# Hybrid attention layer, gates stage: the score matmuls of the next head stand behind the value matmuls of a head

## What is computed

```python
h = rms_norm(x, attn_norm_g)
proj = h @ w_in      # q, k, v of 8 stick-breaking heads and of 8 sparse heads, index heads, gates
o_sb = stick_breaking_attention(q_sb, k_sb, v_sb)
o_ds = indexed_sparse_attention(rope(norm(q_ds)), rope(norm(k_ds)), v_ds, iq, ik, w_ix, topk=64)
merged = sigmoid(g_sb) * (o_sb @ w_branch[:SB_W]) + sigmoid(g_ds) * (o_ds @ w_branch[SB_W:])
x = x + merged @ w_out
u = causal_depthwise_conv(rms_norm(x, ffn_norm_g) @ w_up, conv_w, conv_b)
gate, val = split(u)
return x + (silu(gate) * val) @ w_down
```

## Time and profile before

| | us |
|---|---|
| median of 3 runs | 1438.19 (1438.11 to 1438.35) |
| the profiled execution's time | 1438.27 |
| its span in the trace | 1436.3 |
| PE busy | 1429.9 (100%) |
| DVE busy | 1140.8 (79%) |
| ACT busy | 841.9 (59%) |
| POOL busy | 448.6 (31%) |
| gates stage | 332.7 to some 537 |

### The profile page before, as it was taken

One profiled execution on the slowest core, in us unless ns is written; L12 is line 12 of the kernel. 1 busy time (PEld: TensorE's weight loads), 2 busy tenths in 40 slices (PEclk: granted clock), 3 DMA queues, 4 the chain that ended last, 5 costly groups with the idle time before them and its releaser, 6 DMA issues.

```text
span 1436.3 us, 23630 instructions
## 1 busy us (share of the span) xinstructions
PE 1429.9 (100%) x7570; PEld 1225.7 (85%) x7570; DVE 1140.8 (79%) x1533; ACT 841.9 (59%) x1181; POOL 448.6 (31%) x495
## 2 busy tenths in 40 slices
PE   9999999999999999999999999999999999999999
PEld 7888888888888888888888888888888888888887
DVE  6778998886656656889967777778778778999998
ACT  6645677566767766666665455454554545465553
POOL 2310000423232213650015455655556555200000
PEclk9999999999999999999999999999999999999999
DMA  8665665665554555567666666666666665576664
GB/s 250 188 191 169 204 201 179 201 182 173 158 174 146 173 164 183 183 222 236 187 183 183 190 192 188 178 191 190 199 185 182 188 192 189 193 232 206 201 208 147
DMA packets 121063, 272.24 MB, mean 190 GB/s; under 512 B 10688, under 2 KB 10976, under 8 KB 121008
## 3 DMA queue, kind: packets, MB, share of 16 engines
q1 hardware_dynamic: 119936, 268.99, 61.1%
q0 software_dynamic: 896, 2.42, 0.7%
q10 hardware_dynamic: 176, 0.14, 0.0%
HBM read 269.42 MB, written 2.10 MB: 189 GB/s over the span
## 4 chain that ended last, share of the span: by engine, by line
PE 98%; DVE 1%; DMA 0%; ACT 0%; issue 0%; SPq 0%; DVEq 0%; ACTq 0%
PE bank L2084 97%; DMA y<-in_x 0%; PE bank L2133 0%; DVE lo L1208 0%; PE bank L2345 0%; PE bank L2386 0%; ACT hT L652 0%; DVE y L1754 0%; PE bank L2213 0%; ACT hi L635 0%; DVE lo L1099 0%; DVE msum L1225 0%; DVE msum L1226 0%; ACT hi L713 0%; DVE msum L1235 0%
## 5 line engine op out<-in xcount | busy, mean ns | idle before, releaser
L1099 DVE TENSOR_TENSOR lo<-raw,hi 128x1024 fp32r<-128x1024 f32 (+1 forms) x343 | 446.1, 1306 | 167.3 <-ACT hi L635 166.7
L635 ACT ACTIVATE hi<-raw 128x1024 fp32r<-128x1024 f32 (+1 forms) x343 | 360.2, 1053 | 272.8 <-PE bank L2084 267.7
L2084 PE MATMUL bank<-h2T,hi 128*128 128x512 f32 x1408 | 483.3, 394 | 0.0
L2084 PE MATMUL bank<-h2T,lo 128*128 128x256 f32 x1408 | 376.8, 278 | 0.0
L2084 PEld LDWEIGHTS bank<-h2T,hi 128*128 128x128 f32 x1408 | 257.9, 188 | 53.5
L2084 PE MATMUL bank<-hT,hi 128*128 128x512 f32 (+1 forms) x784 | 273.7, 395 | 0.0
L2084 PEld LDWEIGHTS bank<-h2T,lo 128*128 128x128 f32 x1408 | 264.5, 188 | 7.8
L2084 PE MATMUL bank<-hT,lo 128*128 128x256 f32 (+1 forms) x784 | 213.0, 282 | 0.0
L2048 POOL TENSOR_TENSOR u<-u,rms_row 128x256 f32<-128x256 f32 x88 | 120.8, 1373 | 184.8 <-DVE u L1606 165.8
L2084 PE MATMUL bank<-hi,ffT 128*128 128x512 f32 x576 | 177.4, 389 | 0.0
L2084 PEld LDWEIGHTS bank<-hT,hi 128*128 128x128 f32 (+1 forms) x784 | 144.2, 187 | 29.7 <-DVE hT L1124 0.3
(11 more groups left out here) (299 smaller groups left out, 2025.3 us busy)
## 6 DMA issues: line engine op xcount, KB each, us to landing
raw<-in_w_up SPq DMA_DIRECT2D x176, 512.0 KB, 3.8
raw<-in_w_in SPq DMA_DIRECT2D x160, 512.0 KB, 3.6
raw<-in_w_down SPq DMA_DIRECT2D x88, 512.0 KB, 4.4
raw<-in_w_branch SPq DMA_DIRECT2D x32, 512.0 KB, 3.7
raw<-in_w_out SPq DMA_DIRECT2D x24, 512.0 KB, 5.2
raw4h<-in_w_in SPq DMA_DIRECT2D x8, 512.0 KB, 3.8
raw5h<-in_w_in SPq DMA_DIRECT2D x8, 512.0 KB, 4.1
y<-in_x SPq DMA_DIRECT2D x4, 512.0 KB, 6.6
```

The source lines that it names most:

```text
L635: act.activation(hi[s][:, 0:width], raw[s][:, 0:width], ACT.Copy)\
L1099: dve.tensor_tensor(lo[s][:, 0:width], raw[s][:, 0:width], hi[s][:, 0:width].bitcast(f32), ALU.subtract)\
L2084: return pe.matmul(o, l, r, start=start, stop=stop, skip_group_check=True)
```

## The change

The four score matmuls with their waits become a function, `head_logits`. Only head 0 still runs it behind its chunk 0. At the end of head h, behind the value matmuls, PE runs the scores of head h+1, for h = 0 to 6. The loop over heads is written as head 0, a loop over heads 1 to 6, and head 7. Nothing changes in the code of ACT, DVE, POOL and SP.

```diff
-            with pe.Fori(0, NH) as h:
+            def head_logits(h):
+                pe.wait_ge(staged_qk, 3 * h + 3)
+                pe.wait_ge(qkT_done, 8)
+                mm(B[0][:, 0:S], sb_k[:, 0:P], sb_q[:, :], True, True)
+                mm(B[0][:, S:KEYS], sb_k[:, P:S], sb_q[:, P:S], False, True)\
+                    .then_inc(z_full, 1)
+                mm(B[1][:, 0:P], ds_qk[:, 0:P], ds_qk[:, S:S + P], True, True)
+                mm(B[1][:, P:KEYS], ds_qk[:, P:S], ds_qk[:, S:2 * S], True, True)\
+                    .then_inc(logit_full, 1)
+
+            def gates_body(h, before, more):
...
-                    if j == 0:
-                        pe.wait_ge(staged_qk, 3 * h + 3)
...
+                    if j == 0 and not before:
+                        head_logits(h)
...
+                if more:
+                    head_logits(h + 1)
+
+            gates_body(0, False, True)
+            with pe.Fori(1, NH - 1) as h:
+                gates_body(h, True, True)
+            gates_body(NH - 1, True, False)
```

## The result

| | us |
|---|---|
| changed kernel, median of 6 runs | 1445.54 (1445.35 to 1446.39) |
| kernel before, median of 6 runs | 1438.14 (1437.38 to 1438.35) |
| ratio, 95% interval | 1.0054 (1.0044 to 1.0064) |
| span of the profiled execution, after and before | 1443.7 and 1436.3 |

A forecast was written before the change was run, and what follows sets the result against it. PE was taken as the bound, with 98% of the chain. Seven heads times 0.64 us of stall, 4.5 us, on the profiled 1438.27 gave 1442.8, less 0.08 for the median: 1442.7 us, range 1439.4 to 1445.4.

The forecast's parts named there:

- Slower, the likeliest outcome: Whole kernel: a time slower than 1441.1 us counts as slower; chance 0.74.
- Nothing saved by two stretches: PE, heads 1 to 7: seven fewer switches between kinds of matmul save 0 to 0.35 us in all; taken as 0.
- The shift: ACT after chunk 0: split of j=1 starts 1.31 us later; 0.95 us stay from the split of j=2 to `prob`.
- The margin of 0.14 us: PE's transposes: of 1.09 us between the second `prob` and the first weight load, the 0.95 us shift leaves 0.14.
- DVE ahead of POOL: Heads 1 to 7: DVE's split of j=4 follows `stay_lo` at once, 0.54 us ahead of POOL's second `prob`.
- can hold it up: DVE's split of j=4: the first `prob`, served after `stay_lo`, lengthens it by 0.23 us, bounds 0 and 0.53.
- the rival with both `prob` instructions behind the split: Transposes: DVE goes from `stay_lo` into the split without letting POOL in; 1.01 us a head, 1445.3 us; chance 0.06.
- The earlier trace: Rows used as price: a POOL instruction served between two back-to-back DVE splits; the second took 1.75 us, 0.53 more.
- Chunk 1 and all behind it keep their times: PE, heads 1 to 7: moving the scores ahead makes only chunk 0 end later, by 1.31 us.
- by the rule to the letter: Shared SBUF port: first `prob` holds the split until 398.71, stalling about 0.9 us a head, 6.2 us in all.
- the forecast's 0.64 us a head: Transposes, heads 1 to 7: PE's weight load starts at 400.44 instead of 399.80; bounds 0.41 and 0.94 us.

The follow-up runs named there:

- the waiting split: Changed kernel with one wait more on DVE: its split of j=4 waits until the first of POOL's two `prob` instructions is done; 1440.25 us.
- the last one: Changed kernel with DVE's j=4 split waiting for the first `prob`, plus an extra transpose in heads 0 to 6 and ahead of the branch stage; 1438.98 us.
- The late ACT: Kernel before, PE's order untouched, with four extra `abs` instructions on ACT ahead of `soft` in all 8 heads, results not used; 1446.10 us.
- The run with the gap: Changed kernel with four two-column reciprocals on DVE between `stay_lo` and the split of j=4, results not used; 1443.97 us.
- the run with `prob` on VectorE: Changed kernel with the scaling of `prob` moved from POOL to DVE, behind `stay_lo`; 1440.29 us.
- the remedies: Changed kernel with the waiting split, 1440.25 us; with a transpose ahead of the branch stage, 1444.69; in the heads, 1446.43; combined, 1439.20 and 1438.98.

## Why the prediction was wrong

The time, 1445.54 us, lies 0.14 us above the range of 1439.4 to 1445.4, less than the runs differ among themselves (one of the six, 1445.35, is inside); the forecast itself was 1442.7, 2.8 us lower. Slower, the likeliest outcome, came. By its steps:

- **Nothing saved by two stretches.** Right to 0.02 us a head: the best heads with the new order take 25.71 us against 25.73.
- **The shift.** 1.31 us at the split of j=1, 0.95 at that of j=2: right, and 0.93 at `prob`.
- **The margin of 0.14 us.** Right, measured in head 1 of the run with the waiting split, and again (0.14) in heads 2 to 7 of the last one.
- **DVE ahead of POOL.** Right: its split starts 15.35 us behind the values, forecast 15.36. The late ACT with the scores in their old place and the waiting split with the scores in the new one show that lateness and this order, not the place of the scores as such, make the wait.
- **The step that failed: that the first `prob` "can hold it up" and is served between `stay_lo` and the split.** The split was not held at all, and the first `prob` was: the rival with both `prob` instructions behind the split, to which I gave 0.06 and 1445.3 us. The earlier trace rows was the wrong row to lean on. There the POOL instruction, another operation, had been waiting 1.1 us; here it starts 0.17 us ahead of the split. The first `prob` takes 0.39 us from the split's end (398.66 + 1.22 to 398.49 + 1.77), and 0.72 alone. So by my estimate some 0.33 us pass from its start until it needs the port, by which time the split has it. The run with the gap fits: with the split 0.42 us behind its start, `prob` goes through. This is argued from lengths and not shown, and it holds for the first `prob`, which starts from idle. The second follows it without a pause, and the same working gives 0.13 us (0.92 alone, 0.79 from the split's end in head 0): it went through with only 0.09 us (before) and 0.14 us (waiting split) ahead of the split. A head lost 0.89 us by this, not 0.64: 7 x 0.89 = 6.2 of the 7.4 us.
- **"Chunk 1 and all behind it keep their times"** was wrong too, and the forecast has no term for it. Chunks 1 to 4 of heads 1 to 7 run at 353.4 ns a pair instead of 346.7, and so does the branch stage, whose code isn't touched. In the heads it costs nothing, since PE waits at the transposes for the other chain anyway (some 0.2 of the 0.89 us is slow spacing in place of waiting). In the branch stage it costs 105.26 - 103.96 = 1.3 us. 6.2 + 1.3 = 7.5 us against 7.4.

Two numbers of the prediction come near the measured ones by chance. The rival's 1445.3 us rests on 1.01 us a head, since it took 0.47 us for the part behind the split where 0.39 was measured: 0.8 us too much in the heads against 1.3 us that it lacks in the branch stage. And the 0.9 us a head, 6.2 in all, "by the rule to the letter" are for a split that is held, which it wasn't; from the prediction's own terms that case comes to 398.71 + 1.22 + 0.79 + 0.05 - 399.80 = 0.97 us a head, 6.8 in all.

Without the second item the time would have been 1444.2 us, inside the range; with the forecast's 0.64 us a head and the second item, 1438.1 + 4.5 + 1.3 = 1443.9.

What sets the spacing is not settled. It isn't the shape of the code, nor the wait alone (the run with `prob` on VectorE has no wait and the slow spacing), nor the scores next to chunk 0 (one head of that run is fast), nor the new order as such (the run with the late ScalarE has the order of before and a slow branch stage). One transpose more, 0.11 us, turned it off in the branch stage and in the heads, turned it on in head 1 of the last run, and changed nothing in the kernel before. In every run it lasted until PE stopped or ran another kind of matmul. That it depends on where the stream of matmuls falls in time is a guess that no run here shows.

## What to carry to other kernels

Before matmuls are moved ahead of a chunk, ask who waits for that chunk's end, and follow that engine's queue to the next thing that PE needs. A margin must be held against the chain's shift and also against the order in which two engines reach a shared port: here 0.93 us of lateness would have fitted into the margin of 1.09 us, and so would the 1.05 us by which the order at the port held `prob`; together they cost 0.89 us a head. Where such a conflict is the cause, one wait that keeps the old order takes it away: with the waiting split 2.8 us are left of the 7.4, and none of the remedies made the new order faster than the old. And rows used as a price should agree in when the instruction arrives, not in its kind alone.

## What I had not expected of the hardware

- Two spacings of the same stream of matmuls at a granted clock of 1.00: 346.7 and 353.5 ns for a pair of 512 and 256 columns. The difference is 1.9%, stays over a stage of 90 us, and was switched in the changed kernel by a single matmul of 0.11 us ahead of it. The cause is open.
- To start first is not to have the port. GpSimd's first scaling of `prob` lost with 0.17 us ahead of the split (1.77 us) and went through with 0.42 us (0.72 us); the second, right behind the first, went through with 0.09 us. From the lengths I estimate that the first needs the port some 0.33 us after its start, the second 0.13.
- The 256-column `prob` doesn't hold VectorE for its whole length. It runs 0.92 us, and a split that starts 0.14 us behind it takes 1.40 us instead of 1.22, where a hold to its end would have made it 2.0. The Trainium skill ("SBUF — State Buffer", section "Who interferes with whom") gives the port to the first for the whole instruction. The split that keeps `prob` out until its end agrees, the 1.40 us do not.
